# Expert blocks turned by VectorE in 32x32 squares, with the experts' matrices loaded by quarters in another row order

## The reference

```python
def routed_experts(x, expert_ids, gates, wg, wu, wd):
    # rows sorted by expert, each expert's segment padded to whole blocks
    def run_block(args):
        tok, gate, e = args
        xb = x_pad[tok]
        hdn = jax.nn.silu(xb @ wg[e]) * (xb @ wu[e])
        return (hdn @ wd[e]) * gate[:, None]
```

## Time and profile before

| engine | busy us | share of the span |
|---|---|---|
| TensorE (PE) | 2798.6 | 93% |
| weight loads (PEld) | 1640.7 | 55% |
| VectorE (DVE) | 1423.0 | 47% |
| ScalarE (ACT) | 888.2 | 30% |
| GpSimd (POOL) | 416.7 | 14% |

### The profile page before, as it was taken

One profiled execution on the slowest core, in us unless ns is written; L12 is line 12 of the kernel. 1 busy time (PEld: TensorE's weight loads), 2 busy tenths in 40 slices (PEclk: granted clock), 3 DMA queues, 4 the chain that ended last, 5 costly groups with the idle time before them and its releaser, 6 DMA issues. The chain is left out here.

```text
span 3002.4 us, 81057 instructions
## 1 busy us (share of the span) xinstructions
PE 2798.6 (93%) x33765; PEld 1640.7 (55%) x33766; DVE 1423.0 (47%) x3553; ACT 888.2 (30%) x1898; POOL 416.7 (14%) x633
## 2 busy tenths in 40 slices
PE   6998999999999989999998799958999999999988
PEld 3432445455454557887787455524555555555543
DVE  3246356555566647777777344561222222222218
ACT  2347244344344434444444122210000000000006
POOL 0000000000000001121123000003222222222223
PEclk8999999999999989999999799979999999999999
DMA  8641124223232396556553785555896588768858
GB/s 296 217 142 43 50 86 136 74 106 119 99 127 107 119 252 162 161 156 183 160 151 90 242 295 196 218 202 183 302 336 252 202 303 310 282 247 297 293 198 341
DMA packets 377451, 580.55 MB, mean 193 GB/s; under 512 B 56526, under 2 KB 240774, under 8 KB 374184
## 3 DMA queue, kind: packets, MB, share of 16 engines
q1 hardware_dynamic: 327176, 486.12, 47.2%
q0 software_dynamic: 18832, 70.53, 6.7%
q10 hardware_dynamic: 31248, 21.08, 2.4%
HBM read 412.03 MB, written 165.60 MB: 192 GB/s over the span
## 5 line engine op out<-in xcount | busy, mean ns | idle before, releaser
L523 PE MATMUL pj_P<-normed,pj_wc 128*128 128x448 f32 (+2 forms) x1600 | 594.8, 519 | 0.9 <-ACT pj_stage L656 0.9
L2714 PE MATMUL moe_PG<-wgu,moe_xT 128*32 128x256 f32 x9600 | 550.7, 381 | 0.0
L523 PEld LDWEIGHTS pj_P<-normed,pj_wc 128*128 128x128 f32 x1600 | 295.8, 190 | 259.5 <-issue 243.6
L2714 PEld LDWEIGHTS moe_PG<-wgu,moe_xT 128*32 128x32 f32 x9600 | 297.0, 110 | 206.6 <-issue 26.8
L2544 DVE TENSOR_TENSOR moe_sg<-moe_sg,moe_PG 128x128 f32<-128x128 f32 x150 | 43.1, 288 | 556.0 <-ACT moe_sg L2593 556.0
L2725 PE MATMUL moe_PTY<-wd,moe_hT 128*32 128x256 f32 x4800 | 286.5, 379 | 0.6 <-DVE moe_hT L2549 0.6
L2593 ACT ACTIVATE moe_sg<-moe_PG 128x128 f32<-128x128 f32 x150 | 41.8, 278 | 793.3 <-PE moe_PG L2714 793.3
L2132 PE MATMUL merge_PO<-merge_w,merge_mT 128*128 128x512 f32 x544 | 240.0, 599 | 0.6 <-ACT merge_mT L2178 0.6
L2725 PEld LDWEIGHTS moe_PTY<-wd,moe_hT 128*32 128x32 f32 x4800 | 155.9, 110 | 103.5 <-DVE moe_y L2537 0.7
L2132 PEld LDWEIGHTS merge_PO<-merge_w,merge_mT 128*128 128x128 f32 x544 | 102.7, 191 | 125.1 <-issue 124.4
L2636 POOL DMA_INDIRECT moe_xg<-scratch_h,moe_row x154 | 149.9, 974 | 125.7 <-POOL moe_xc L2649 114.9
(11 more groups left out here) (434 smaller groups left out, 4231.6 us busy)
## 6 DMA issues: line engine op xcount, KB each, us to landing
wgu<-in_w_gate SPq DMA_DIRECT2D x32, 2048.0 KB
wgu<-in_w_up SPq DMA_DIRECT2D x32, 2048.0 KB
wd<-in_w_down SPq DMA_DIRECT2D x32, 2048.0 KB
scratch_y_rows<-merge_zeros SPq DMA_DIRECT2D x51, 512.0 KB, 4.8
scratch_hk<-pj_hk SPq DMA_DIRECT2D x16, 1344.0 KB, 5.8
normed<-scratch_hk SPq DMA_DIRECT2D x32, 640.0 KB, 7.9
re_hkf<-scratch_hk SPq DMA_DIRECT2D x32, 640.0 KB
scratch_y_rows<-moe_y ACTq DMA_DIRECT2D x604, 32.0 KB
```

What stands on the lines that cost most here:

```text
L523: ins = eng.matmul(bank[:, 0:wp], wc[:, j, k, :], hT[:, k, k0:k0 + wp], start=(k == 0), stop=(k == KD - 1), skip_group_check=True)
L2714: ins = eng.matmul(PG[32 * q:32 * q + 32, 0, 0:256].rearrange("p (a b) -> p a b", a=2), x_rows, wgu[p][:, :, k, 128 * q:128 * q + 128], st ...
```

## The change

`load_expert` issues four DMAs for each matrix, one for each quarter of 32 partitions. The order of the rows changes with it: before, partition p held rows p, p + 128, ... of the matrix; now partition 32q + c holds rows 256q + 32k + c (for the down matrix 128q + 32k + c). The runs are as long as before. With that order the weights of step k must hold, on partition 32q + c, feature 256q + 32k + c of the block's rows, and that is what transposing each 32x32 square of `xg` in place gives. So VectorE turns `xg` straight into `xT` (`turn_x`) and `hid` straight into `hT`, by one instruction each. TensorE's three transposes of a block, ScalarE's copy to `xT`, VectorE's copy to `hT`, GpSimd's copy to `xc` and the buffer `xc` are gone, and with them the semaphores between them.

```diff
     for n in matrices:
-        src = ...[0, ds(e, 1)].rearrange("e (k p) n -> p (e k) n", p=128)
-        eng.dma_start(gate_up[:, n, :, :] if n < 2 else down[:, :, :], src).then_inc(loaded[n], 16)
+        src = ...[0, ds(e, 1)].rearrange("e (q k c) n -> q c (e k) n", q=4, c=32)
+        for q in range(4):
+            rows = slice(32 * q, 32 * q + 32)
+            eng.dma_start(gate_up[rows, n, :, :] if n < 2 else down[rows, :, :], src[q]).then_inc(loaded[n], 16)
...
 # VectorE
+                def turn_x(g, p, times):
+                    eng.wait_ge(ev(f"gathered{p}"), times)
+                    eng.transpose(xT[:, :], xg[p][:, :]).then_inc(ev("x_turned"), 1)
+                turn_x(0, 0, 16)
                 with eng.Fori(0, n_pairs) as i:
                     for p in range(2):
                         g = i * 2 + p
+                        eng.wait_ge(ev("gu_made"), g + 1)
+                        turn_x(g + 1, 1 - p, i * 16 + 16 + 16 * p)
                         eng.wait_ge(ev("sigmoid_made"), g + 1)
...
+                        eng.wait_ge(ev("hid_ready"), g + 1)
+                        eng.wait_ge(ev("y_made"), g + 1)
+                        eng.transpose(hT[:, :], hid[:, :]).then_inc(ev("hT_kept"), 1)
                         keep_y(g + 1, 1 - p, i)
-                        eng.wait_ge(ev("h_turned"), g + 1)
-                        eng.tensor_copy(hT[:, :], PH[:, 0, 0:128]).then_inc(ev("hT_kept"), 1)
 # ScalarE
-                        eng.wait_ge(ev("x_turned"), g + 3)
-                        eng.copy(xT[:, :, :], PT[:, :, :]).then_inc(ev("xT_kept"), 1)
 # GpSimd
-                        eng.tensor_copy(xc[:, :], xg[p][:, :]).then_inc(ev("x_moved"), 1)
                         eng.wait_ge(ev("row_ready"), i * 2 + (p + 3))
+                        eng.wait_ge(ev("x_turned"), i * 2 + (p + 1))
                         gather(p)
 # TensorE
-                def gate_up(g, p):
-                    eng.wait_ge(ev("xT_kept"), g + 1)
+                def gate_up(g, p, first=False):
+                    eng.wait_ge(ev("x_turned"), g + 1)
+                    if not first:
+                        eng.wait_ge(ev("hid_ready"), g)
                     for k in range(KD):
...
-                        turn(g + 1)
-                        turn_hid(g - 1)
                         gate_up(g, p)
                         down(g, p)
...
-                        eng.wait_ge(loaded[p][matrix], i * 16 + 16)
+                        eng.wait_ge(loaded[p][matrix], i * 64 + 64)
```

More of the change, by code:

```diff
@@ L1987, in load_expert @@
     for n in matrices:
-        src = t[("w_gate", "w_up", "w_down")[n]][0, ds(e, 1)].rearrange("e (k p) n -> p (e k) n", p=128)
-        eng.dma_start(gate_up[:, n, :, :] if n < 2 else down[:, :, :], src).then_inc(loaded[n], 16)
+        src = t[("w_gate", "w_up", "w_down")[n]][0, ds(e, 1)].rearrange("e (q k c) n -> q c (e k) n", q=4, c=32)
+        for q in range(4):
+            rows = slice(32 * q, 32 * q + 32)
+            eng.dma_start(gate_up[rows, n, :, :] if n < 2 else down[rows, :, :], src[q]).then_inc(loaded[n], 16)
 def merge(nc, t, expert, gates, wgu, wd, loaded, held, held_in, tables):
@@ L2368, in experts @@
         xg = [sb(f"xg{p}", [128, 256]) for p in range(2)]
-        xc = sb("xc", [128, 256])
-        xT = sb("xT", [128, 2, 128])
+        xT = sb("xT", [128, 256])
         sg = sb("sg", [128, 128])
@@ L2377, in experts @@
         PH = ctx.enter_context(nc.psum_tensor("moe_PH", [128, 2, 512], F32))
-        PT = PTY[:, 0, 0:256].rearrange("p (a b) -> p a b", b=128)
         PY = PTY[:, 1, 0:256]
@@ L2585, in _ @@
                 n_blocks = total(eng)
-                eng.wait_ge(ev("x_turned"), 1 + 1)
-                eng.copy(xT[:, :, :], PT[:, :, :]).then_inc(ev("xT_kept"), 1)
                 n_pairs = n_blocks // 2
@@ L2593, in _ @@
                         eng.activation(sg[:, :], PG[:, 0, 0:128], ACT.Sigmoid).then_inc(ev("sigmoid_made"), 1)
-                        eng.wait_ge(ev("x_turned"), g + 3)
-                        eng.copy(xT[:, :, :], PT[:, :, :]).then_inc(ev("xT_kept"), 1)
                         store_y(g, 1 - p)
                 store_y(n_pairs * 2, 1)
-                eng.wait_ge(ev("xT_kept"), n_pairs * 2 + 1)
                 eng.wait_ge(ev("y0_out"), n_pairs * 64 + 64)
@@ L2641, in _ @@
                     gather(p)
-                n_pairs = (n_blocks + 2) // 2
+                n_pairs = n_blocks // 2
                 with eng.Fori(0, n_pairs) as i:
@@ L2646, in _ @@
                         eng.tensor_copy(row[:, p:p + 1], rows[:, ds(i * 2 + (p + 2), 1)]).then_inc(ev("row_ready"), 1)
+                        eng.wait_ge(ev("row_ready"), i * 2 + (p + 3))
                         eng.wait_ge(ev("x_turned"), i * 2 + (p + 1))
-                        eng.sem_inc(ev("move_begun"), 1)
-                        eng.tensor_copy(xc[:, :], xg[p][:, :]).then_inc(ev("x_moved"), 1)
-                        eng.wait_ge(ev("row_ready"), i * 2 + (p + 3))
-                        eng.wait_ge(ev("x_moved"), i * 2 + (p + 1))
                         gather(p)
@@ L2667, in _ @@
                 eng.wait_ge(ev("member_ready"), 1)
-                for name in ("x_turned", "y_made", "y_kept"):
+                for name in ("y_made", "y_kept"):
                     eng.sem_inc(ev(name), 1)
@@ L2692, in _ @@
                 eng.wait_ge(ev("rows_ready"), 1)
-                def turn(g, first=False):
-                    eng.wait_ge(ev("x_moved"), g + 1)
+                def gate_up(g, p, first=False):
+                    eng.wait_ge(ev("x_turned"), g + 1)
                     if not first:
[L2698 to L2706, removed]
-                def gate_up(g, p):
-                    eng.wait_ge(ev("xT_kept"), g + 1)
+                        eng.wait_ge(ev("hid_ready"), g)
                     for k in range(KD):
-                        x_rows = xT[:, k % 2, 32 * (k // 2):32 * (k // 2) + 32]
                         for q in range(4):
-                            ins = eng.matmul(PG[32 * q:32 * q + 32, 0, 0:256].rearrange("p (a b) -> p a b", a=2), x_rows, wgu[p][:, :, k, 128 * q:128 * q + 128],
+                            ins = eng.matmul(PG[32 * q:32 * q + 32, 0, 0:256].rearrange("p (a b) -> p a b", a=2), xT[:, 32 * k:32 * k + 32], wgu[p][:, :, k, 128 * q:128 * q + 128],
                                              start=(k == 0), stop=(k == KD - 1))
@@ L2748, in next_expert @@
                     down(g, 1 - p)
-                    eng.wait_ge(loaded[p][2], i * 16 + 16)
+                    eng.wait_ge(loaded[p][2], i * 64 + 64)
                     eng.sem_inc(ev("down_begun"), 1)
-                turn(0, first=True)
                 before, first, second = blocks_of_pair(eng, 0)
                 for matrix in range(3):
[L2755 to L2758, removed]
+                    eng.wait_ge(loaded[0][matrix], 64)
+                gate_up(before, 0, first=True)
                 rest_of_expert(before, first, 0)
@@ L2768, in _ @@
                 n_blocks = total(eng)
-                turn_hid(n_blocks - 1)
                 down(n_blocks, 1)
```

## The result

The changed kernel takes 3173.1 us, the median of 4 runs (3164.2 to 3177.3), beside 3001.9 for the kernel before on the same chip: a ratio of 1.0562, 95% interval 1.0542 to 1.0582. It is some 170 us slower. The prediction had 3096.6 and a range up to 3205, so the direction and the range hold and the size is too small. The profiled execution has a span of 3162.3 us, where the steps of the prediction add up to 3099.4: 63 us are to be found (77 by the medians; the profiled execution is the fastest of the four).

The account below looks back on a forecast made before the run. TensorE bound the kernel before; half-rate loads were to bind the changed one. Loops +91, merge +9 and start -3 gave +97 us, a span of 3099.4, less 2.8 for the median: 3096.6 us, range 2955 to 3205.

Parts of the forecast that it names:

- rivals B: Experts' loops: a matrix's four quarters overlap in the queue, near full rate, loads stay hidden; 2916 us; chance 0.13.
- rival D: Experts' loops: loads stay hidden but turn_x outlasts its cover, say 1.2 us, giving back 45 us; 2961; chance 0.03.
- The stores: Experts' loops: stores of 128 KB a block don't write to SBUF and can use time in which an engine waits.
- The clock falls: Experts' loops: a clock falling in the waits at changes of expert, named as a sign of being wrong, without a price.
- The load's rate: Experts' loops: loads into 32 partitions move at 215 GB/s, 29.3 us an expert, a little above half rate.
- The gather: Experts' loops: each block's gather adds 0.15 us to the loads, within 0 to 0.31; 0.7 us for an expert.
- The idle queue: Experts' loops: the few experts of six and seven blocks leave the load queue idle for about 10 us.
- the sign that I named: Experts' loops: gaps between w_gate issues about 30 us for short experts, 37 for those of seven blocks.
- The first two come early, with time behind them: Merge: the first two of six loads, each 5 us longer, have time to spare; merge as a whole loses 9 us.
- SP's issues: Experts' loops: 12 DMAs an expert instead of 3, at 0.4 us each, 3.6 us more, covered by SP's waiting.
- rival A: The forecast itself: loads at about half rate bind the experts' loops; own range 3005 to 3207 us; chance 0.74.
- Rival C: Experts' loops: part overlap, 240 to 280 GB/s, short experts wait, 25 to 55 of 83 us given back; chance 0.10.

Follow-up runs that it names:

- a_full_width: The changed kernel with each expert matrix loaded again by one DMA over all 128 partitions, in the old row order: 2918.6 us, 0.9726 of the kernel before.
- a_half_down: The changed kernel with half of each block's down left out and all DMAs kept: 3174.1 us, 1.0576 of the kernel before.
- a_merge_wide: The changed kernel with only merge's six loads (experts 0 and 1) at full width: 3154.9 us, 1.0504 of the kernel before.
- a_one_store: The changed kernel with one of the four stores of `y` in each block: 3174.1 us, 1.0547 of the kernel before.
- b_spread: The kernel before with each matrix loaded by four DMAs, each taking every fourth partition: 3001.5 us, 0.9995 of the kernel before.
- c_wide: The changed kernel's VectorE turns with full-width loads, `h2`'s features permuted in merge and gate_up's columns taken in pieces of 32: 2915.3 us, 0.9706 of the kernel before.
- b_quarters: The kernel before, old row order, with each matrix loaded by four DMAs of 32 neighbouring partitions: 3190.6 us, 1.0625 of the kernel before.
- b_halves: The kernel before with each matrix loaded by two DMAs of 64 neighbouring partitions: 3194.0 us, 1.0639 of the kernel before.
- b_half_spread: The kernel before with four DMAs for each matrix, each taking every second partition of one half: 3200.5 us, 1.0665 of the kernel before.

## Why the prediction was right, and where its sum fell short

**Right.** The bound moves from TensorE to the loads, because a narrow target halves the rate (rivals B and C would have needed 240 GB/s and more, and the loads have some 204). The block's period is 5.18 us, 5.27 predicted. turn_x takes 0.445 us, inside 0.42 to 0.62, and costs nothing (`a_full_width`, so rival D falls). The Trainium skill's 311 ns for a 128x128 turn, page "VectorE: DVE Perf Modes", section "The three transpose paths", is for bf16; the trace has the same 311 ns for float32. The estimate made from it by doubling, 0.62 us, is too high for 256 columns: 0.445. The start gains 2.7 us, 3 predicted. The stores are free within the noise. The clock falls at the changes of expert, as the prediction feared, and costs nothing (`a_half_down`).

**Short by 63 us.** The mechanism held; sizes of the sum did not. By place, in the profiled execution:

| place | predicted | measured | difference |
|---|---|---|---|
| loops, first gate_up to last copy of `y` | 967 | 3072.9 - 2048.3 = 1024.6 | +58 |
| end of merge | 1993.8 + 9 | 2008.35 | +5.6 |
| start of experts, tail | 39.7, 89.5 | 39.9, 89.4 | 0 |

**The load's rate was mis-sized.** The loops less the 26.4 us to the first issue (2074.65 - 2048.28), 15 for x1 and 17.6 for the last blocks leave 965.6 us for 30 experts, 32.2 each. Of this the gather's 5 blocks x 0.25 are 1.2, so a load takes 31.0 us: 203 GB/s. The window 2200 to 2900 gives 135.3 MB without x1, in 700 us less 25 for the gathers and 12 for x1: 204. I had taken 215, "a little above the half", by the argument that longer transfers do better. They do not: half of the 395 to 418 of the earlier trace rows is 198 to 209, and the long streams lie in it. The 240 and 215 GB/s of the earlier trace rows are windows of 1 us, too short to stand against that. This is 30 x 1.7 = +51 us.

**The gather was mis-sized**: 0.25 us for a block where I took 0.15, 30 x 0.5 = +15.

**The idle queue was not there**: I added 10 us for experts of six and seven blocks. Up to two experts' loads stand in the queue, so a load that is issued late still finds the engines at work on the one before: the rate is 240 GB/s in both windows of 200 us above, at a clock of 0.97 and of 0.89. -10 us. With 2 us for the first issue these three make the +58. They are read from one execution; with the same loads in the loops others have 1029.4 us (`a_half_down`), 1036.2 (`a_merge_wide`) and 1041.4 (`a_one_store`) where this one has 1024.6, so each term holds to some 10 us and no better. For the same reason the sign that I named failed: the gaps between issues are not about 30 us for short experts and 37 for those of seven blocks, but run from 21 to 46. An issue row tells when the queue took the DMA and not when it moved. Nor does TensorE wait for wgu 30 times: it is 9 waits for `w_up` and 23 for `w_down`, 3.8 us on average.

**In merge one step failed.** "The first two come early, with time behind them" looked at the loads' own deadline. What counts is what stands behind them in the same queue: the input of the next tile, 10.4 us late. The end costs 6.9, where I had 9. 17 instead of 9 in all; 3 us of it don't show in the table, since the parts before happened to end that much earlier in this execution.

**SP's issues** were costed at 0.4 us each. They are 2.4 us in the median for `w_up`, and four of them can take over 12 us, presumably since SP has to wait for room in its queue (no run here shows how deep it is). In the loops no cost of it is seen, since the DMA engines have work all the time (a share of 1.06 from 2200 to 2900); in merge it is part of the step that failed, as the four of `w_up` kept SP from 1731.01 to 1738.75.

**Slips in the working.** The 26.2 us that rival A names for 240 GB/s leaves the gather out; its 3005 goes with 26.9. Rival C gives back 25 to 55 us of 83, which is 2941 to 2971 and not 2942 to 3005. The chance of "slower", 0.75, is more than the 0.74 of the only rival that is slower. None of them moves the forecast.

## What to carry to other kernels

Before a load is cut up by partitions, look at which halves of the partitions each piece reaches: a piece inside 0 to 63 or 64 to 127 moved at about half the rate here, and cutting by every fourth partition (`b_spread`), or loading whole and permuting elsewhere (`c_wide`), avoided it. A share of the DMA engines near 1 with far fewer GB/s than usual was the sign of it. When a transfer becomes slower, cost also what is queued behind it on the same queue, even where the transfer itself has time to spare.

## What the runs showed of the hardware that was not expected

- Half of the partitions gives about half of the rate. In the changed kernel the loads have 203 to 204 GB/s once the gathers and x1 are taken off, against 395 to 418 at full width. Before that is taken off they have 201, and 195 to 197 in `b_quarters` (32 neighbouring partitions), `b_halves` (64 neighbouring) and `b_half_spread` (32 alternate ones of one half), which cost 6.3% to 6.7% of the whole time; four transfers over every fourth partition cost nothing measurable (`b_spread`, 0.9995) and reach 398 GB/s.
- The same stretch of time holds a half-rate load and stores out of SBUF with no loss that shows (`a_one_store`: nothing beyond some 12 us of noise for 96 KB a block in 150 blocks), but a gather into all partitions adds some 0.25 of its 0.31 us.
- In the changed kernel issuing one DMA on SP takes up to 6.4 us, and 2.4 us in the median for `w_up`, where in the kernel before the median for `w_up` is 0.5 us.
- VectorE turns 128x128 float32 in 32x32 squares in 311 ns and 128x256 in 445 ns, 134 ns more for twice the columns; that is hardly more than its copy of 128x256 takes (424 ns).
